# Moving the split weights 16 bytes against the activations in a two-layer decoder trunk

## The chip, the cores and the metric

The kernel runs on one core of one Trainium2 chip. The metric is the device time of one execution in microseconds (us). The median of three runs of the kernel before is 1382.09 us (1382.05 to 1382.2).

## What is computed

Two residual layers on x of 256 tokens by 1024 channels, batch 1, all in float32:

```
h = rms_norm(x)
layer 0: p = h @ w_in_ab; gMLP gating on some columns, dilated attention on the others
         x = x + concat(...) @ w_out_ab
         x = x + (silu(h' @ wg) * (h' @ wu)) @ wd             # width 2816
layer 1: p = h @ w_in_cd; block attention (12 heads) and a short convolution
         x = x + concat(...) @ w_out_cd
         out = sum over 8 experts of gate[:, e] * swiglu(h', wg[e], wu[e], wd[e])   # width 3584
         x = x + out                                          # each token has 2 of 8 gates
```

The last stage is the largest: eight experts, three matrices each of 1024 x 3584 floats.

## The kernel before, in words

**Three products for one.** A matmul of plain float32 operands is replaced by three with operands of the type float32r. Each weight tile and each activation is split in a high part (a copy rounded to float32r) and a low part (the rest). `three` (L724 to L728) issues high x high (L726), high x low (L727) and low x high (L728) into the same PSUM bank. Its first operand is the stationary one (128 columns, loaded by LDWEIGHTS), the second the moving one. In the profile's rows the moving operand is named first: `psum<-w_hi,xg_hi` has weights moving, activations stationary.

**The weights' way.** SP loads tiles of 4096 floats a partition (2 MB) into `raw_ring`, which has 7 slots, in a fixed order (L547 to L581). A tile is worked on in four units of 1024 floats. For each unit ACT writes the high part into `w_hi` (L388; L409 in the expert stage), DVE subtracts it and writes the low part into `w_lo` (L396, L414), and PE multiplies. `w_hi` and `w_lo` have 4 buffers each; ACT waits until PE has used the unit four before (`unit_used`), and SP reloads a slot when DVE has split its last unit (`lo_ready`).

**Who multiplies what.** In the projections (`project`, L788; `first_tile`, L762), the output projections (`ab_unit`, `out_units`, `out_last`) and the down product of the feed-forward (`down`, L1185) 512 (at times 256) columns of weights move past 128 stationary columns of `act` or `ffn_h`. The feed-forward reads its input from `ffn_in_hi/lo`: at its opening (L1199 to L1210) it is stationary and 512 columns of weights move; from then on (L1213 to L1227) 128 columns of weights are stationary and 256 columns of `ffn_in` move. The convolution (`conv_half`, L1005) is of that second form, with `act` moving. In the expert stage (`job`, L1320; eight jobs, one for each expert, of 7 gate, 7 up and 7 down tiles) 512 columns of weights move, and `xg` (128 gathered tokens) or `moe_hT` is stationary. There `transpose_h` (L1307) turns the hidden rows with transposes whose moving operand is the identity, in `const`; `gather` (L1290) does so with `xg_rows`.

**Where things lie.** All addresses in SBUF are laid out by hand. `keep` (L190) places buffers one behind the other and rounds each up to 32 bytes; `at` gives an address outright:

```
        raw = keep("raw_ring", [RING, TILE])
        wh = keep("w_hi", [SPLITS, UNIT], F32R)
        wl = keep("w_lo", [SPLITS, UNIT], F32R)
        xres = keep("x_residual", [TT, D])
        cst = keep("const", [C_COLS])
...
        R0 = place[0] + PHASE + 256
        act_hi = at("act_hi", [KD, SEQ], F32R, R0)
        ffn_hi = at("ffn_in_hi", [KD, SEQ], F32R, R0 + FFN_PHASE)
```

`xg` and `moe_h` start at R0 plus multiples of 4096, and `ffn_h`, `moe_hT`, `xg_rows`, `probs` at R0 plus 16384 plus multiples of 256. Each step of a loop over k, c or a buffer number moves an operand by a multiple of 256 bytes, so two operands keep their distance modulo 256 bytes through a whole stage.

From the start of `raw_ring` to R0 there are 169,952 bytes of buffers, plus PHASE = 32, plus 256: 170,240, which is 665 x 256. `w_hi` starts 114,688 = 448 x 256 bytes behind that start. So activations and weights lie at the same place modulo 256, and `ffn_in` (FFN_PHASE = -192) 64 bytes past them.

Of the kernel before, what the change touches and what calls it, by code (L numbers as in the profile page):

```python
# [24 lines left out]
F32R = mybir.dt.float32r  # L25
# [26 lines left out]
UNIT = 1024  # L52
SPLITS = 4
# [1 line left out]
SLAB = 512  # L55


PHASE, FFN_PHASE = 32, -192
SLABS = FE // SLAB
JOB_TILES = 3 * SLABS  # L60
JOB_UNITS = JOB_TILES * TILE // UNIT
# [109 lines left out]
def decoder_trunk(nc, x, norm_mix, norm_ffn, w_in_ab, gmlp_v_gain, gmlp_ws, gmlp_bs, dil_q_gain, dil_k_gain,  # L171
# [10 lines left out]
    with ExitStack() as ctx:  # L182
# [4 lines left out]
        def at(name, shape, dt, offset):  # L187
            return nc.alloc_sbuf_tensor_at(name, [P, *shape], dt, offset=offset)

        def keep(name, shape, dt=F32):  # L190
            size = int(np.prod(shape)) * (2 if dt == BF16 else 4)
            t = at(name, shape, dt, place[0])
            place[0] += (size + 31) // 32 * 32
            return t

        raw = keep("raw_ring", [RING, TILE])
        wh = keep("w_hi", [SPLITS, UNIT], F32R)
        wl = keep("w_lo", [SPLITS, UNIT], F32R)
        xres = keep("x_residual", [TT, D])
        cst = keep("const", [C_COLS])  # L200
        colpar = keep("col_params", [48])
# [2399 lines left out]
```

## Time and profile before

| | |
|---|---|
| median of three runs | 1382.09 us |
| profiled execution, its own time | 1382.9 us |
| its span, first to last instruction | 1381.1 us |
| PE busy | 1366.9 us (99%) |
| DVE busy | 1194.4 us (86%) |
| ACT busy | 1026.2 us (74%) |
| read from HBM | 425.09 MB, 313 GB/s over the span |

The profile gives each engine's busy time. The matmuls are pipelined, and each one's duration holds its way through the array, so they overlap: 512 columns show 389 to 394 ns while the next one starts 227 ns later. For the pace of TensorE the starts of neighbours in the timeline are to be read, not the durations. PEld is the load of stationary operands, beside PE.

### The profile page before, as it was taken

How to read it: one execution, taken by the hardware profiler on the slowest of the kernel's cores; microseconds unless marked ns; L12 is line 12 of the kernel's file. 1: busy time of each engine (PE TensorE's matmuls, PEld its weight loads, DVE VectorE, ACT ScalarE, POOL GpSimd, SP SyncE). 2: the span in 40 equal slices, each digit the busy share in tenths (PEclk: the TensorE clock that was granted, in tenths of full speed). 3: DMA queues.
4: the chain of work that ended last, by engine and by line, in shares of the span. 5: the costliest groups of instructions: out<-in, count | busy, mean ns of one | idle time of the engine just before them, and what ended most of it. 6: DMA issues, size and time to landing. Idle time of an engine off the chain costs nothing.

```text
span 1381.1 us, 20276 instructions
## 1 busy us (share of the span) xinstructions
PE 1366.9 (99%) x6985; PEld 1150.9 (83%) x6985; DVE 1194.4 (86%) x1517; ACT 1026.2 (74%) x1262; POOL 86.2 (6%) x67
## 2 busy tenths in 40 slices
PE   9999999999999999999999999999999999999998
PEld 7778999988988788888888888888888888888886
DVE  5876555568959999999999999999999999999998
ACT  5666444456758788888887887888888888888877
POOL 1020000000320000000100100010010001001000
PEclk9999999999999999999999999999999999999999
DMA  9944543643658999999999999999999999999980
GB/s 347 356 151 154 183 153 122 231 136 122 245 183 331 362 375 348 391 392 377 357 394 380 342 396 393 377 355 393 382 352 394 389 376 354 393 376 351 394 328 30
DMA packets 183760, 430.28 MB, mean 312 GB/s; under 512 B 5449, under 2 KB 13301, under 8 KB 183712
## 3 DMA queue, kind: packets, MB, share of 16 engines
q1 hardware_dynamic: 181408, 423.86, 82.7%
q0 software_dynamic: 2304, 5.78, 2.1%
q8 instruction: 30, 0.49, 0.1%
q14 instruction: 18, 0.15, 0.0%
HBM read 425.09 MB, written 7.34 MB: 313 GB/s over the span
## 4 chain that ended last, share of the span: by engine, by line
PE 93%; DVE 5%; ACT 1%; issue 1%; DVEq 0%; ACTq 0%
PE psum L726 29%; PE psum L728 29%; PE psum L727 29%; PE psum L1313 2%; DVE w_lo L414 1%; DVE w_lo L396 1%; PE psum L1294 0%; PE psum L758 0%; PE psum L1157 0%; PE psum L859 0%; DVE probs L2078 0%; PE psum L1000 0%; PE psum L891 0%; PE psum L877 0%; PE psum L968 0%
## 5 line engine op out<-in xcount | busy, mean ns | idle before, releaser
L414 DVE TENSOR_TENSOR w_lo<-raw_ring,w_hi 128x1024 fp32r<-128x1024 f32 x674 | 812.3, 1223 | 48.3 <-ACT w_hi L409 4.0
L409 ACT ACTIVATE w_hi<-raw_ring 128x1024 fp32r<-128x1024 f32 x675 | 715.3, 1063 | 169.0 <-PE psum L728 168.4
L726 PE MATMUL psum<-w_hi,xg_hi 128*128 128x512 f32 x896 | 353.4, 394 | 1.1 <-DVE w_lo L414 1.0
L728 PE MATMUL psum<-w_hi,xg_lo 128*128 128x512 f32 x896 | 349.3, 390 | 0.0
L727 PE MATMUL psum<-w_lo,xg_hi 128*128 128x512 f32 x896 | 348.9, 389 | 0.0
L396 DVE TENSOR_TENSOR w_lo<-raw_ring,w_hi 128x1024 fp32r<-128x1024 f32 x124 | 151.7, 1230 | 78.7 <-ACT w_hi L388 77.7
L388 ACT ACTIVATE w_hi<-raw_ring 128x1024 fp32r<-128x1024 f32 x124 | 129.9, 1057 | 95.1 <-PE psum L728 94.9
L728 PEld LDWEIGHTS psum<-w_hi,xg_lo 128*128 128x128 f32 x896 | 168.2, 188 | 35.7
L726 PEld LDWEIGHTS psum<-w_hi,xg_hi 128*128 128x128 f32 x896 | 168.3, 188 | 34.9 <-issue 1.4
L727 PEld LDWEIGHTS psum<-w_lo,xg_hi 128*128 128x128 f32 x896 | 168.4, 188 | 33.6
L726 PE MATMUL psum<-w_hi,moe_hT_hi 128*128 128x512 f32 x448 | 176.1, 393 | 0.1
L728 PE MATMUL psum<-w_hi,moe_hT_lo 128*128 128x512 f32 x448 | 174.6, 390 | 0.0
L727 PE MATMUL psum<-w_lo,moe_hT_hi 128*128 128x512 f32 x448 | 174.3, 389 | 0.0
L728 PEld LDWEIGHTS psum<-w_hi,moe_hT_lo 128*128 128x128 f32 x448 | 84.1, 188 | 17.9
L726 PEld LDWEIGHTS psum<-w_hi,moe_hT_hi 128*128 128x128 f32 x448 | 84.1, 188 | 17.4 <-issue 0.5
L727 PEld LDWEIGHTS psum<-w_lo,moe_hT_hi 128*128 128x128 f32 x448 | 84.2, 188 | 17.1
L726 PE MATMUL psum<-w_hi,act_hi 128*128 128x512 f32 (+1 forms) x224 | 86.0, 384 | 2.9 <-DVE w_lo L396 2.1
L728 PE MATMUL psum<-w_hi,act_lo 128*128 128x512 f32 (+1 forms) x224 | 84.0, 375 | 0.0
L727 PE MATMUL psum<-w_lo,act_hi 128*128 128x512 f32 (+1 forms) x224 | 83.9, 374 | 0.0
L726 PE MATMUL psum<-ffn_in_hi,w_hi 128*128 128x256 f32 x288 | 80.9, 281 | 0.0
L727 PE MATMUL psum<-ffn_in_lo,w_hi 128*128 128x256 f32 x288 | 80.4, 279 | 0.0
L728 PE MATMUL psum<-ffn_in_hi,w_lo 128*128 128x256 f32 x288 | 80.4, 279 | 0.0
(286 smaller groups left out, 1355.9 us busy)
## 6 DMA issues: line engine op xcount, KB each, us to landing
raw_ring<-in_moe_w_gate SPq DMA_DIRECT2D x56, 2048.0 KB, 10.3
raw_ring<-in_moe_w_up SPq DMA_DIRECT2D x56, 2048.0 KB, 10.8
raw_ring<-in_moe_w_down SPq DMA_DIRECT2D x56, 2048.0 KB, 10.7
raw_ring<-in_ffn_w_gate SPq DMA_DIRECT2D x5, 2048.0 KB, 7.9
raw_ring<-in_ffn_w_up SPq DMA_DIRECT2D x5, 2048.0 KB, 9.3
raw_ring<-in_ffn_w_down SPq DMA_DIRECT2D x5, 2048.0 KB, 10.1
raw_ring<-in_w_in_ab SPq DMA_DIRECT2D x4, 2048.0 KB, 16.2
raw_ring<-in_w_in_cd SPq DMA_DIRECT2D x4, 2048.0 KB, 8.0
```

The source lines that it names most:

```text
L388: act.activation(part(wh, u, w), raw_unit(u), ACT.Copy).then_inc(hi_ready, 1)
L396: dve.tensor_tensor(part(wl, u, w), raw_unit(u), part(wh, u, w).bitcast(F32), ALU.subtract).then_inc(lo_ready, 1)
L409: act.activation(wh[:, v % SPLITS, :], moe_raw(i, q), ACT.Copy).then_inc(hi_ready, 1)
L414: dve.tensor_tensor(wl[:, v % SPLITS, :], moe_raw(i, q), wh[:, v % SPLITS, :].bitcast(F32), ALU.subtract).then_inc(lo_ready, 1)
L726: pe.matmul(out_, sh, mh_, start=start, stop=False)
L727: pe.matmul(out_, sh, ml_, start=False, stop=False)
L728: return pe.matmul(out_, sl, mh_, start=False, stop=stop)
L1313: mm = pe.transpose(ps[:, 4, c * P:(c + 1) * P], mh[:, i % 2, c * P:(c + 1) * P], ident)
```

## The change

`w_hi` and `w_lo` become slices of one allocation, `w_split`, that begin LINE = 4 floats (16 bytes) into it. With 4 floats of padding at either end it is 32 bytes longer than the two were, so all that `keep` places behind it (`x_residual`, `const`, the parameters, the masks) lies 32 bytes further on. PHASE goes from 32 to 0, which makes up for it: R0 stays where it was. FFN_PHASE goes from -192 to -128: `ffn_in` moves up by 64 bytes. No instruction is added, removed or reordered.

```
-PHASE, FFN_PHASE = 32, -192
+PHASE, FFN_PHASE, LINE = 0, -128, 4
...
-        wh = keep("w_hi", [SPLITS, UNIT], F32R)
-        wl = keep("w_lo", [SPLITS, UNIT], F32R)
+        split = keep("w_split", [2 * SPLITS * UNIT + 2 * LINE], F32R)
+        wh = split[:, LINE:LINE + SPLITS * UNIT].rearrange("p (s f) -> p s f", s=SPLITS)
+        wl = split[:, LINE + SPLITS * UNIT:LINE + 2 * SPLITS * UNIT].rearrange("p (s f) -> p s f", s=SPLITS)
```

Starts modulo 256 bytes, counted from the start of `raw_ring`:

| | before | after |
|---|---|---|
| `raw_ring` | 0 | 0 |
| `w_hi`, `w_lo` | 0 | 16 |
| `x_residual`, `const` | 0 | 32 |
| `act`, `xg`, `moe_h`, `moe_hT`, `ffn_h` | 0 | 0 |
| `ffn_in` | 64 | 128 |
| `act`, `xg`, `moe_hT`, `ffn_h` less weights | 0 | -16 |
| `ffn_in` less weights | +64 | +112 |

## Rows read from the trace of the kernel before

**Rows 1.** The page: span, busy time, share and instructions of each engine

```profile
span 1381.1 us, 20276 instructions
PE 1366.9 (99%) x6985; PEld 1150.9 (83%) x6985; DVE 1194.4 (86%) x1517; ACT 1026.2 (74%) x1262; POOL 86.2 (6%) x67
```

**Rows 2.** The page: the chain that ended last, by engine

```profile
PE 93%; DVE 5%; ACT 1%; issue 1%; DVEq 0%; ACTq 0%
```

**Rows 3.** Groups by line, shapes apart, weights moving: busy us, mean ns | idle before

```profile
L726 PE MATMUL psum<-w_hi,xg_hi 128*128 128x512 f32 x896 | 353.4, 394 | 1.1 <-DVE w_lo L414 1.0
L726 PE MATMUL psum<-w_hi,moe_hT_hi 128*128 128x512 f32 x448 | 176.1, 393 | 0.1
L726 PE MATMUL psum<-w_hi,act_hi 128*128 128x512 f32 x192 | 76.7, 399 | 2.9 <-DVE w_lo L396 2.1 <-issue 0.8
L726 PE MATMUL psum<-w_hi,ffn_h_hi 128*128 128x512 f32 x88 | 34.5, 392 | 0.0
L726 PE MATMUL psum<-w_hi,ffn_in_hi 128*128 128x512 f32 x32 | 12.8, 399 | 0.2 <-DVE ffn_in_lo L1880 0.2
```

**Rows 4.** The same view, weights stationary or 256 columns, and the transposes

```profile
L726 PE MATMUL psum<-ffn_in_hi,w_hi 128*128 128x256 f32 x288 | 80.9, 281 | 0.0
...
L726 PE MATMUL psum<-act_hi,w_hi 128*128 128x256 f32 x48 | 14.5, 303 | 0.2 <-ACT p_v L1673 0.2
...
L726 PE MATMUL psum<-w_hi,act_hi 128*128 128x256 f32 x32 | 9.3, 290 | 0.0
...
L1313 PE MATMUL psum<-const,moe_h 128*128 128x128 f32 x224 | 33.5, 271 | 0.0
```

**Rows 5.** PE timeline, expert stage: start us, us; 14 evenly spaced matmuls between

```profile
902.75 0.39 PE L726 MATMUL psum<-w_hi,xg_hi 128*128 128x512 f32 x1
...
906.15 0.39 PE L726 MATMUL psum<-w_hi,xg_hi 128*128 128x512 f32 x1
```

**Rows 6.** PE timeline, the feed-forward's opening; 16 matmuls between

```profile
119.82 0.39 PE L727 MATMUL psum<-w_lo,ffn_in_hi 128*128 128x512 f32 x1
...
123.79 0.39 PE L726 MATMUL psum<-w_hi,ffn_in_hi 128*128 128x512 f32 x1
```

**Rows 7.** PE timeline, feed-forward with stationary weights; 26 matmuls between

```profile
137.78 0.28 PE L728 MATMUL psum<-ffn_in_hi,w_lo 128*128 128x256 f32 x1
...
140.96 0.28 PE L728 MATMUL psum<-ffn_in_hi,w_lo 128*128 128x256 f32 x1
```

**Rows 8.** PE timeline, convolution; 9 matmuls between

```profile
379.14 0.28 PE L727 MATMUL psum<-act_lo,w_hi 128*128 128x256 f32 x1
...
380.34 0.28 PE L728 MATMUL psum<-act_hi,w_lo 128*128 128x256 f32 x1
```

**Rows 9.** Timeline, all engines: a matmul and the next load of a stationary operand

```profile
902.98 0.39 PE L727 MATMUL psum<-w_lo,xg_hi 128*128 128x512 f32 x1
902.98 0.19 PEld L728 LDWEIGHTS psum<-w_hi,xg_lo 128*128 128x128 f32 x1
```

**Rows 10.** PE timeline: four transposes in the expert stage and what follows

```profile
914.32 0.60 PE L1313 MATMUL psum<-const,moe_h 128*128 128x128 f32 x4
914.67 0.48 PE L726 MATMUL psum<-w_hi,xg_hi 128*128 128x512 f32 x1
```

**Rows 11.** Three stretches of the expert stage: length, then busy us by engine

```profile
600.00:800.00 200.00, 200.00 (x918) 165.79 (x918) 189.63 (x195) 164.75 (x184) 15.79 (x6) 1.00 1.02 373
800.00:1000.00 200.00, 200.00 (x915) 165.77 (x914) 188.98 (x192) 162.95 (x176) 9.57 (x4) 1.00 1.03 382
1000.00:1200.00 200.00, 200.00 (x915) 165.71 (x913) 190.14 (x199) 164.95 (x186) 14.16 (x5) 1.00 1.02 376
```

**Rows 12.** Groups by line from 600 to 1200 us: the two splits

```profile
L414 DVE TENSOR_TENSOR w_lo<-raw_ring,w_hi 128x1024 fp32r<-128x1024 f32 x425 | 513.0, 1224 | 31.3 <-ACT w_hi L409 1.8
L409 ACT ACTIVATE w_hi<-raw_ring 128x1024 fp32r<-128x1024 f32 x424 | 449.5, 1063 | 105.7 <-PE psum L728 105.4
```

**Rows 13.** The page: DMA issues, KB each, us to landing

```profile
raw_ring<-in_moe_w_gate SPq DMA_DIRECT2D x56, 2048.0 KB, 10.3
```

**Rows 14.** POOL groups: a write that starts 4 bytes off, and one that doesn't

```profile
L665 POOL TENSOR_TENSOR conv_y<-conv_y,row_params 128x255 f32<-128x255 f32 x2 | 1.5, 772 | 0.2
...
L637 POOL TENSOR_TENSOR p_uv<-p_uv,small 128x256 f32<-128x256 f32 x2 | 1.2, 615 | 47.6 <-DVE small L2019 47.5
```

## The prediction, made before the changed kernel was run

> **What bounds the kernel now.** I read the busy shares first, then the chain, the groups, and at last the timeline. TensorE is busy for 1366.9 of 1381.1 us [rows 1], and 93% of the chain that ended last is PE [rows 2]. Its groups hardly wait: the largest, 896 matmuls, idled 1.1 us in all [rows 3]. In three stretches of 200 us of the expert stage PE has no gap, at granted clock 1.00, that is 2.4 GHz [rows 11]. So the time is the number of matmuls times the distance from one start to the next, and only that distance can be moved by a change that adds and removes no instruction.
>
> The durations don't show it, the starts do. Between the two matmuls of [rows 5] lie 15 distances in 3.40 us: 226.7 ns for 512 columns. With 256 columns and the same placement it is 1.20 us for 10, 120.0 ns [rows 8]. The difference, 106.7 ns for 256 columns, is the pure cost of a column (0.417 ns, one cycle at 2.4 GHz); both forms carry 13.3 ns on top. The kernel before happens to hold other placements too. At the opening of the feed-forward the same form of matmul reads a stationary operand 64 bytes past the weights, and takes 3.97 us for 17 distances, 233.5 ns [rows 6]: 6.8 ns more, 20.2 on top. Later the weights are stationary and the input moves, so that the stationary one lies 64 bytes short: 3.18 us for 27, 117.8 ns [rows 7], 2.2 ns less than [rows 8], 11.1 on top. The load of the next stationary operand starts in the same hundredth of a microsecond as the matmul that it runs beside [rows 9], so both read SBUF together. Below, "distance" of an address is that of the stationary operand less that of the moving one, modulo 256.
>
> **The change, part by part.**
>
> (a) Weights moving, 512 columns, distance from 0 to -16 bytes. [Rows 3] has 896 + 448 + 192 + 88 triples whose stationary operand moves by this: 1624 x 3 = 4872 matmuls. At 226.7 ns they are 1104 us, 80% of the span, all of it on the path. No row has -16. The price comes from the neighbours: from 0 to +64 it rises by 6.8 ns, 0.106 ns a byte; carried on to the other side, 16 bytes give -1.7 ns. From 0 to -64 (256 columns) it falls by only 2.2 ns, so the line must flatten somewhere; evenly spread, 16 bytes would give -0.55 ns, and -2.2 at once if it is a step. I take -1.7, from the rows of the same form: -8.3 us. Ends: -2.2 ns, -10.7 us, and, since nothing excludes that 0 is the best place, the +6.8 ns of the worst row, +33.1 us.
>
> The Trainium skill (TensorE: Matmul & The Clock Gate, Step-by-step: what each phase is for) says that the moving and the stationary operand have a read port each and that the load takes no bandwidth from the running matmul. By that rule the change is worth nothing; this trace speaks against it, since 226.7 and 233.5 ns stand for one form of matmul at two placements.
>
> (b) The feed-forward's opening, distance from +64 to +112: 32 x 3 = 96 matmuls [rows 3]. The same line gives +5.1 ns, +0.5 us. Ends: -0.7 us (back to the 226.7 of [rows 5]) and +1 us (twice the line).
>
> (c) The rest of the feed-forward, weights stationary, distance from -64 to -112: 288 x 3 = 864 matmuls of 256 columns [rows 4]. The nearest row is their own, 117.8 ns; I take no change. Ends: another 48 bytes at 2.2 / 64 ns each, -1.4 us; or the 20.2 ns on top of [rows 6] instead of 11.1, +9.1 ns, +7.9 us.
>
> (d) Convolution, 48 x 3 with the distance from 0 to +16, and 32 x 3 projection matmuls of 256 columns with -16 [rows 4]: 144 x 1.7 = +0.2 us and 96 x 1.7 = -0.2 us, together nothing; no more than 1.3 us either way at 6.8 and 2.2 ns.
>
> (e) Transposes move the identity, in `const`, which goes 32 bytes up, while most of their stationary operands stay: four of them lie in 0.35 us to the next matmul [rows 10]. There are 224 of this line [rows 4], and I count about 420 in all. Zero, since nothing in the trace prices their placement; 6.8 ns each would be +2.9 us, 2.2 ns each -0.9 us.
>
> (f) ACT's and DVE's splits read `raw_ring` at 0 and write 16 bytes past a multiple of 32. They lie beside PE. From 600 to 1200 us DVE is busy for 189.63 + 188.98 + 190.14 = 568.8 of 600 us [rows 11], 425 splits in it [rows 12]: 1338 ns a unit against PE's 1412. So 74 ns more on each split of 1224 cost nothing, and PE 5.2% faster would still be fed. Below that cover each further ns costs one on some 670 units. The only rows with a start off 32 bytes are POOL's, 772 ns for 255 elements against 615 for 256 in another operation [rows 14], on an engine whose times are rough. A quarter more on DVE's split would add 306 - 74 = 232 ns a unit, +155 us; I take zero, as POOL's two rows are different operations.
>
> (g) DMA: SP's loads don't move. A tile takes 10.3 us to land [rows 13] and is asked for up to seven tiles ahead, and a tile is 4 x 1.41 = 5.6 us of PE; a pace 0.7% faster asks for 380 GB/s where the stretches show 373 to 382 [rows 11]. Cover stays.
>
> Sum: -8.3 + 0.5 + 0 + 0 = -7.8 us. Against the profiled execution's own 1382.9 us that is 1375.1; the median of the runs is 0.8 lower, so I forecast 1374.3 us. Own range 1371 to 1379.
>
> **The rivals.**
>
> *Zero is the best place* (slower). What costs the 13.3 ns may be smallest where both reads start in step, and rise to both sides. For it: +64 is dearer. Against it: -64 isn't, though with half the columns. It decides as soon as a start-to-start distance in the expert stage is above 227.3 ns (0.2% of the run spread over 4872). Price: 1.7 ns the other way is +8.3 us, 1390 us, and up to 1415 at the 233.5 ns of [rows 6].
>
> *A larger step down.* The 13.3 ns on top may be a meeting of the two reads at the same place, which a shift of 16 bytes avoids in large part. Half of it gone would be -6.7 ns, -32.6 us, 1350 us. For it: with 11.1, 13.3 and 20.2 the amount does depend on placement. Against it: 64 bytes short saved only 2.2. DVE's 5.2% of cover would just hold (6.7 of 226.7 is 3.0%).
>
> By the Trainium skill (TensorE: Matmul & The Clock Gate, Back-to-back issue gap) a matmul of 512 columns costs 512 / 2.4 + 2.5 = 215.8 ns; 10.9 ns less on 4872 would be -53 us, some 1329 us, an estimate from that page alone. The rows here show nothing below 11.1 ns on top.
>
> *It does nothing.* The cost might go by coarser steps than 16 bytes, so that -16 reads like 0: 1382 us. For it: the trace shows only distances in steps of 64. Against it: +64 and -64 differ from 0 in both directions, so there is a slope somewhere. The rule of the Trainium skill cited under (a) (TensorE: Matmul & The Clock Gate, Step-by-step: what each phase is for) gives this same time.
>
> *DVE becomes the bound* by the placement in (f): over 1400 us. Nothing but POOL's rows speaks for it.
>
> **How the numbers follow.** Forecast 0.40; larger step down 0.15; nothing, or within 0.2% (2.8 us, about what a measurement of this kernel tells from no change), 0.17; zero is best 0.25; DVE 0.03. Faster by over 0.2% is 0.40 + 0.15 = 0.55, the same 0.17, slower 0.28. The 8-in-10 range reaches down into the larger step, to 1354, and up through +8.3 us to about +3 ns a matmul, 1397; some 0.07 lies below and 0.12 above.
>
> **What would show it.** Right: starts in the expert stage 225.0 ns apart where they were 226.7, the opening of the feed-forward at about 238, its later part still near 118, splits still 1224 and 1063 ns, PE without gaps. Wrong: 228 ns or more in the expert stage (zero was best), 222 or less (a larger step), a PE that waits for `w_lo` with splits over 1300 ns (f), or gains in the expert stage given back in the feed-forward (c).

## The result, and the profile after

The changed kernel takes 1404.1 us (1404.01 to 1404.47, 5 runs) against 1382.2 us for the kernel before in the same session: a ratio of 1.0158, 95% interval 1.0147 to 1.0168. It is 22 us slower; the prediction said 8 us faster, range 1354 to 1397.

The page of the changed kernel; the lines of the source stand one lower than before, and both split buffers now carry the name `w_split`:

```profile
span 1402.7 us, 20276 instructions
PE 1389.1 (99%) x6985; PEld 1154.6 (82%) x6985; DVE 1195.6 (85%) x1517; ACT 1026.9 (73%) x1262; POOL 59.0 (4%) x67
...
PE 94%; DVE 4%; ACT 1%; issue 1%; DVEq 0%; ACTq 0%
...
L727 PE MATMUL psum<-w_split,xg_hi 128*128 128x512 f32 x896 | 357.2, 399 | 0.9 <-DVE w_split L415 0.8
...
raw_ring<-in_moe_w_gate SPq DMA_DIRECT2D x56, 2048.0 KB, 10.2
```

The same count of instructions, PE on 94% of the chain where it was 93%, and no wait of PE that was not there in [rows 1 to 3]. The splits, by line over the stretch from 600 to 1200 us:

```profile
L415 DVE TENSOR_TENSOR w_split<-raw_ring,w_split 128x1024 fp32r<-128x1024 f32 x417 | 504.1, 1223 | 40.3 <-ACT w_split L410 33.5
L410 ACT ACTIVATE w_split<-raw_ring 128x1024 fp32r<-128x1024 f32 x416 | 441.3, 1064 | 113.8 <-PE psum L729 113.0
```

1223 and 1064 ns against 1224 and 1063 [rows 12]: ACT and DVE don't notice the 16 bytes. They wait more, ACT on PE and DVE on ACT. The same three stretches as in [rows 11], with busy us and number of instructions of each engine:

```profile
600.00:800.00 200.00, 200.00 (x900) 163.17 (x899) 186.66 (x192) 161.74 (x181) 6.72 (x6) 1.00 1.01 367
800.00:1000.00 200.00, 200.00 (x898) 163.05 (x897) 186.01 (x191) 160.42 (x175) 5.08 (x4) 1.00 1.01 375
1000.00:1200.00 200.00, 200.00 (x899) 163.03 (x898) 187.25 (x196) 161.84 (x181) 5.09 (x5) 1.00 1.01 369
```

The granted clock is 1.00 (2.4 GHz) as before and PE has no gap, but it starts 900, 898 and 899 matmuls where it started 918, 915 and 915. So each is further from the next. In the PE timeline (start us, us) of the expert stage, with 15 evenly spaced matmuls between:

```profile
910.79 0.40 PE L727 MATMUL psum<-w_split,xg_hi 128*128 128x512 f32 x1
...
914.50 0.40 PE L728 MATMUL psum<-w_split,xg_hi 128*128 128x512 f32 x1
```

3.71 us for 16 distances, 231.9 ns, against 226.7 [rows 5]. The feed-forward's opening (19 matmuls between) and its later part (29 between):

```profile
119.19 0.39 PE L729 MATMUL psum<-w_split,ffn_in_lo 128*128 128x512 f32 x1
...
123.86 0.39 PE L728 MATMUL psum<-w_split,ffn_in_hi 128*128 128x512 f32 x1
...
149.82 0.28 PE L728 MATMUL psum<-ffn_in_lo,w_split 128*128 128x256 f32 x1
...
153.42 0.28 PE L728 MATMUL psum<-ffn_in_lo,w_split 128*128 128x256 f32 x1
```

4.67 us for 20 is 233.5 ns, exactly [rows 6]; 3.60 us for 30 is 120.0 ns, 2.2 more than [rows 7].

Read to the nanosecond, the starts show more. All 6985 matmuls come in the same order in both kernels, so their start times can be subtracted one by one: the changed kernel is 0.6 us late at the end of layer 0's mixer, 0.5 after the opening of the feed-forward, 3.4 at its end, 4.4 at the start of the expert stage, and 21.6 at its end. In that stage the distances are not random. Once a few matmuls have passed behind a break, before the change they go 227, 226, 227 without end, and after it 235, 235, 230, 227, 235, 235, 230, 227: a cycle of four matmuls, mean 231.7. The few matmuls of run-in cost the kernel before some 36 ns in each of 57 stretches, and the changed kernel 2 ns.

### The profile page after: what moved, and what is told of

Read it like the earlier page. It is cut to its first block, busy times and chain, and to the rows that moved or that the text cites. A ratio compares the mean times of both kernels' runs of the same rounds, so it can differ in the third digit from the quotient of the medians.

```text
span 1402.7 us, 20276 instructions
## 1 busy us (share of the span) xinstructions
PE 1389.1 (99%) x6985; PEld 1154.6 (82%) x6985; DVE 1195.6 (85%) x1517; ACT 1026.9 (73%) x1262; POOL 59.0 (4%) x67
## 4 chain that ended last, share of the span: by engine, by line
PE 94%; DVE 4%; ACT 1%; issue 1%; DVEq 0%; ACTq 0%
PE psum L727 30%; PE psum L729 29%; PE psum L728 29%; PE psum L1314 2%; DVE w_split L397 1%; PE psum L1295 0%; PE psum L759 0%; PE psum L1158 0%; PE psum L860 0%; DVE probs L2079 0%; PE psum L1001 0%; PE psum L892 0%; DVE rope_tmp L466 0%; DVE p_qk L468 0%; DVE rope_tmp L460 0%
## 5 line engine op out<-in xcount | busy, mean ns | idle before, releaser
L415 DVE TENSOR_TENSOR w_split<-raw_ring,w_split 128x1024 fp32r<-128x1024 f32 x674 | 813.7, 1223 | 63.6 <-ACT w_split L410 52.6
L410 ACT ACTIVATE w_split<-raw_ring 128x1024 fp32r<-128x1024 f32 x675 | 715.8, 1064 | 185.5 <-PE psum L729 184.4
L727 PE MATMUL psum<-w_split,xg_hi 128*128 128x512 f32 x896 | 357.2, 399 | 0.9 <-DVE w_split L415 0.8
L729 PE MATMUL psum<-w_split,xg_lo 128*128 128x512 f32 x896 | 353.3, 394 | 0.0
L728 PE MATMUL psum<-w_split,xg_hi 128*128 128x512 f32 x896 | 353.1, 394 | 0.0
L397 DVE TENSOR_TENSOR w_split<-raw_ring,w_split 128x1024 fp32r<-128x1024 f32 x124 | 151.4, 1227 | 82.6 <-ACT w_split L389 81.7
L389 ACT ACTIVATE w_split<-raw_ring 128x1024 fp32r<-128x1024 f32 x124 | 130.3, 1058 | 99.2 <-PE psum L729 98.8
L729 PEld LDWEIGHTS psum<-w_split,xg_lo 128*128 128x128 f32 x896 | 168.5, 188 | 39.0
L727 PEld LDWEIGHTS psum<-w_split,xg_hi 128*128 128x128 f32 x896 | 168.6, 188 | 38.2 <-issue 1.3
L728 PEld LDWEIGHTS psum<-w_split,xg_hi 128*128 128x128 f32 x896 | 168.7, 188 | 37.1
L727 PE MATMUL psum<-w_split,moe_hT_hi 128*128 128x512 f32 x448 | 178.0, 397 | 0.1
L729 PE MATMUL psum<-w_split,moe_hT_lo 128*128 128x512 f32 x448 | 176.6, 394 | 0.0
L728 PE MATMUL psum<-w_split,moe_hT_hi 128*128 128x512 f32 x448 | 176.6, 394 | 0.0
L727 PEld LDWEIGHTS psum<-w_split,moe_hT_hi 128*128 128x128 f32 x448 | 84.3, 188 | 19.2 <-issue 0.5
L728 PEld LDWEIGHTS psum<-w_split,moe_hT_hi 128*128 128x128 f32 x448 | 84.3, 188 | 18.8
L727 PE MATMUL psum<-w_split,act_hi 128*128 128x512 f32 (+1 forms) x224 | 86.5, 386 | 2.5 <-DVE w_split L397 1.6
L728 PE MATMUL psum<-w_split,act_hi 128*128 128x512 f32 (+1 forms) x224 | 84.6, 378 | 0.0
```

What stands on the lines that cost most here:

```text
L389: act.activation(part(wh, u, w), raw_unit(u), ACT.Copy).then_inc(hi_ready, 1)
L397: dve.tensor_tensor(part(wl, u, w), raw_unit(u), part(wh, u, w).bitcast(F32), ALU.subtract).then_inc(lo_ready, 1)
L410: act.activation(wh[:, v % SPLITS, :], moe_raw(i, q), ACT.Copy).then_inc(hi_ready, 1)
L415: dve.tensor_tensor(wl[:, v % SPLITS, :], moe_raw(i, q), wh[:, v % SPLITS, :].bitcast(F32), ALU.subtract).then_inc(lo_ready, 1)
L727: pe.matmul(out_, sh, mh_, start=start, stop=False)
L728: pe.matmul(out_, sh, ml_, start=False, stop=False)
```

## The experiments

In the kernels among them the activations or the weights are moved by constants only; instructions and their order stay. The four runs of TensorE alone (`map512`, `map256`, `breaks`, `breaks256`) leave the whole computation out. Where an activation had to lie off 32 bytes, it became a slice of a buffer that begins lower, as the change does it for the weights. Below, a placement is written (moving, stationary), both starts in bytes modulo 256 counted from `raw_ring`. Where 512 columns of weights move past `act`, `xg`, `moe_hT` or `ffn_h`, the kernel before is (0, 0) and the changed one (16, 0). "Stretch" is a run of matmuls of one form between two transposes or other breaks.

**Weights or distance?**

```
act_back16  -PHASE, FFN_PHASE = 32, -192          +PHASE, FFN_PHASE = 16, -176
both_up16   -PHASE, FFN_PHASE, LINE = 0, -128, 4  +PHASE, FFN_PHASE, LINE = 16, -192, 4
act_up16    -PHASE, FFN_PHASE = 32, -192          +PHASE, FFN_PHASE = 48, -192
act_back64  -PHASE, FFN_PHASE = 32, -192          +PHASE, FFN_PHASE = -32, -128
```

> The kernel before with the activations moved instead of the weights: weights at 0 modulo 256, all operands of the activations 16 bytes lower (distance -16 as after the change), ffn_in kept 64 bytes past the weights as before. Distance theory (only stationary less moving counts): 231.7 ns from start to start in the expert stage as after the change, feed-forward opening 233.5 and its later part 117.8 as before; about 1382 + 20 = 1402 us. Line-start theory (weights that begin off a multiple of 32 bytes are dear to stream): 226.7 ns and 1382 us, as the weights are back on 0. If any operand off 32 bytes costs: also near 1402, so the next run has to tell.

Measured: 1383.13 us, ratio to before 1.0002 (0.9993 to 1.0012). The very distance of the change, with the weights at 0, costs next to nothing: by the start times 0.7 us in the expert stage, where 37 of 57 stretches run at 226.7 ns and 20 at 228.3. That fells the distance theory.

> The kernel after with the activations moved up by 16 bytes too and ffn_in put at +64 less the weights: everything 16 bytes past 0, distance 0. Distance theory: 226.7 ns in the expert stage, 117.8 in the feed-forward, 1382 us. Line-start theory, for weights or for any operand: 231 ns or more, 1400 us or more.

Measured: 1398.02 us, ratio 1.011 (1.0093 to 1.0127). Distance 0, but everything 16 bytes up, and the expert stage goes at 231.8 ns in the mean. Yet the later part of the feed-forward, at (80, 16), ran at 113.3 ns, 4.5 less than in the kernel before, on stationary weights that begin at 16. So weights off 32 bytes are not dear where they stay; for weights that move, the line-start theory still stands here, and w16_act160 below decides on it.

> The kernel before with activations 16 bytes higher (distance +16; ffn_in at +80). Distance theory with 0 as the best place: between 226.7 and 231.7 if the cost rises evenly to +64 (about 228.4 by the line of 0.106 ns a byte), or 231.7 if both sides are alike; 1390 to 1404 us.

Measured: 1405.35 us (one run). At (0, 16) the expert stage holds both 226.7 and 233.3 ns. In its PE timeline, 50 matmuls at even pace stand between the first two rows, 33 between the last two:

```profile
914.73 0.39 PE L736 MATMUL psum<-w_lo,xg_hi 128*128 128x512 f32 x1
...
926.63 0.39 PE L736 MATMUL psum<-w_lo,xg_hi 128*128 128x512 f32 x1
926.86 0.39 PE L737 MATMUL psum<-w_hi,xg_lo 128*128 128x512 f32 x1
927.09 0.60 PE L1322 MATMUL psum<-const,moe_h 128*128 128x128 f32 x4
927.45 0.47 PE L735 MATMUL psum<-w_hi,xg_hi 128*128 128x512 f32 x1
...
928.21 0.39 PE L735 MATMUL psum<-w_hi,xg_hi 128*128 128x512 f32 x1
...
935.92 0.39 PE L736 MATMUL psum<-w_lo,moe_hT_hi 128*128 128x512 f32 x1
```

11.90 us for 51 distances is 233.3 ns; then come four transposes; then 7.71 us for 34, 226.8 ns. The placement is the same on both sides (the last row is already a down product, with `moe_hT` at 16 like `xg`). The pace changed across the transposes. Inside a stretch, behind its first few matmuls, it changes in none of the 57 of this run. This is the key of the study: a placement can have two paces, and a break can lead from one to the other.

> The kernel before with activations 64 bytes lower (distance -64; ffn_in kept at +64). If the expert stage follows the 256-column rows (2.2 ns less at -64 than at 0), 224.5 ns and about 1371 us. If 0 is the best place and -16 cost 5.0 ns, more than 231.7 ns at -64, 1404 us or more. If the cost depends on multiples of 64 only for the placement of lines, 226.7 ns and 1382 us.

Measured: 1390.64 us (one run), 228.8 to 228.9 ns in all 57 stretches of the expert stage. None of the three numbers.

**TensorE alone.** Next the disputed cost was measured by itself.

> A kernel of its own that leaves the whole computation out: TensorE alone multiplies triples as in the expert stage (512 columns move, 128 are stationary, low parts 16384 and 4096 bytes behind the high ones), 27 matmuls for each of 16 x 16 placements of the moving and the stationary operand in steps of 16 bytes modulo 256, with ACT, DVE and the loads silent. If the cost is made by TensorE's own two reads and hangs on both starts, the map shows the kernels' own paces: 226.7 ns for (moving 0, stationary 0), 231 to 232 for (16, 0) and (16, 16), 232.5 for (0, 16), 228 for (0, 240), 229 for (0, 192), 233.3 for (0, 64), and there are placements below 226. If it is made by ACT's and DVE's accesses beside it, all 256 places give one number, 226.7 or less. If only the distance counts, rows of equal distance agree.

> The same for the form of the feed-forward and the convolution: 128 columns of weights stationary, 256 of the activations moving. If TensorE's own two reads make the cost: 119.7 ns for (moving 0, stationary 0), 117.8 for (64, 0), 119.5 to 119.9 for (128, 16) and (80, 0), 113.4 for (80, 16). If ACT and DVE make it: one number throughout.

Measured: ACT and DVE are silent, DVE is busy for 7.3 us in all, and the paces are there all the same:

```profile
span 1664.4 us, 14478 instructions
...
PE 1642.4 (99%) x7216; PEld 1337.8 (80%) x7216; DVE 7.3 (0%) x1; ACT 13.1 (1%) x15; POOL 0.2 (0%) x4
```

(16, 0) shows 234, 235, 230, 228, the changed kernel's own cycle. (16, 16) shows 228, 232, mean 230.0, which is the pace of 10 of the 57 stretches of both_up16; the others have paces that the next run shows. Some rows of the maps, ns from start to start, mean of 24 distances behind one break:

```
512 columns move    stationary at
moving at     0    16    48    64    80   112   128   160   192   240
    0     227.7 226.7 233.2 233.3 232.0 233.3 233.3 233.3 229.5 228.0
   16     231.5 230.0 227.3 234.7 226.8 227.1 233.2 226.7 231.2 232.2
   64     229.5 231.8 227.7 228.3 233.5 233.2 233.3 233.9 232.2 230.2
  192     233.3 232.3 233.4 232.1 233.3 229.8 228.9 233.4 226.7 233.2

256 columns move
    0     119.9 118.3 122.7 114.0 118.8 120.3 118.8 120.0 117.8 119.9
   16     113.6 117.9 119.8 118.8 113.9 116.6 116.7 114.9 118.1 118.2
   64     117.8 116.7 117.2 119.5 118.3 117.8 114.0 118.8 118.5 118.1
  192     114.0 118.8 119.6 118.6 119.8 118.1 117.8 116.8 119.4 118.3
```

Along a row of the map only the address of the load of the stationary operand differs, down a column only that of the moving one, and the pace changes with either, so both reads have a part in it. A cell is one draw, but the next run confirms this on many: (0, 0), (0, 64) and (16, 0) keep apart in all their stretches. The loads themselves take 187 to 190 ns at every placement of the first form. Two cells missed their forecast clearly: (0, 16) gave 226.7 where 232.5 was expected, and (80, 16) of the second form 118.3 where 113.4 was. The places below 226 ns that were expected are not there either.

Of 256 placements of the first form 12 are under 227.0 and 117 over 233; none is under 226.7. The first form's best is 226.7 / 512, the second's 113.3 / 256: 0.443 ns a column in both, 17/16 of the cycle of 0.417 ns.

**Does a break choose?**

> TensorE alone again, the computation left out: ten placements (moving, stationary), each with 28 stretches of 21 matmuls, and before each stretch a break (one matmul of 64 to 172 columns, every other time behind four transposes). If the start-to-start distance is fixed by the placement, all 28 stretches of a placement settle at one pace. If a break can throw the two reads into another standing pattern, some placements show two or more paces: (0, 16) 226.7 and 233, (0, 240) 226.7 and 228.5, while (0, 0) always comes back to 226.7 and (16, 0) never does (231.7).

Measured, mean of the last 12 distances of each of 28 stretches:

```
placement    paces (stretches)                the kernels' expert stage, stretches of 20 and more
(0, 0)       226.7 to 227.6 (28)              before: 226.7 (57)
(16, 0)      231.6 to 231.7 (28)              after: 231.7 (57)
(0, 240)     228.3 (20), 226.7 (8)            act_back16: 226.7 (37), 228.3 (20)
(0, 16)      233.2, 233.3 (22), 226.7 (6)     act_up16: 233.3 (49), 226.7 (8)
(16, 16)     230.0 (12), 233.3 (12), 231 (4)  both_up16: 231.1 (25), 233.3 (22), 230.0 (10)
(0, 192)     228.8, 228.9 (27), 233.3 (1)     act_back64: 228.9 (57)
(16, 160)    231 (18), 226.7 (10)             w16_act160: 231.1 (34), 226.7 (23)
(0, 64)      233.3 (28)
(80, 96)     236.7 (21), 233.3 (5), 226.7 (2)
(192, 192)   227.5 to 227.7 (15), 226.7 (13)
```

Each kernel runs at the paces that its placement has when TensorE is alone, and at no others; how often it has each differs. (0, 0) always returns to its fast pace (the values up to 227.6 still hold some of the run-in of a stretch of 21), (16, 0) never finds one.

**Three checks inside the kernel.**

```
w16_act160   +PHASE, FFN_PHASE, LINE = 160, -208, 4
after_ffn80  +PHASE, FFN_PHASE, LINE = 0, -176, 4
ffn_up16     +PHASE, FFN_PHASE = 32, -240
```

> The kernel after, weights still at 16, with the activations at 160 and ffn_in at 208. By the maps (moving 16, stationary 160) is 226.7 ns, so the expert stage is as fast as before although the weights begin off 32 bytes; later part of the feed-forward (moving 208, stationary 16) 115.0: 1380 us. If weights at 16 are dear in themselves: 230 ns or more, 1398 us or more.

Measured: 1388.97 us, ratio 1.0046 (1.0031 to 1.0061). Weights at 16 as in the changed kernel, and 16 us of its 22 are gone, by the start times 7.7 before the expert stage and 8.4 in it, where 23 of 57 stretches run at 226.7 and the rest at 231.1. So weights that move from 16 can be streamed at the best pace, and the line-start theory falls too. The opening of the feed-forward, at (16, 208), runs at 226.7 where both kernels had 233.3, and its later part at 113.6. The forecast of 1380 us was missed by 9. The map alone promised too much, since each of its cells is one draw.

> The kernel after with one part undone: ffn_in back to 64 bytes past the weights (that is, at 80), all else as after the change. Expert stage unchanged at 231.7 ns; later part of the feed-forward at 113.4 (as when both lay 16 up) instead of 119.8, 864 matmuls, -5.5 us: 1398.6 us. If (80, 16) falls into its other pattern, 118.4: 1403 us. My first theory (distance alone) gives 117.8, 1402.4 us.

Measured: 1401.61 us, ratio 1.014 (1.0123 to 1.0157), between the two forecasts, and by the start times 3.0 us less than the changed kernel. The expert stage stays at 231.7, so the feed-forward's input is a small part of the loss. The later part ran at 113.3 ns until the first down products came between; the 256-column stretches after them ran at 118.3. In the timeline, 29 matmuls between these two rows of the fast part:

```profile
152.02 0.28 PE L736 MATMUL psum<-ffn_in_hi,w_split 128*128 128x256 f32 x1
...
155.42 0.28 PE L736 MATMUL psum<-ffn_in_hi,w_split 128*128 128x256 f32 x1
```

3.40 us for 30 distances, 113.3 ns. So a change of form can be a break too.

> The kernel before with ffn_in alone moved, from 64 to 16 bytes past the weights; everything else as before. By the maps: later part of the feed-forward at 113.6 ns (moving 16, stationary 0) instead of 117.8, 864 matmuls, -3.6 us; its opening at 226.7 (moving 0, stationary 16) instead of 233.3, 96 matmuls, -0.6 us: 1378 us. If the pace also hangs on the break before, the later part could stay at 118 to 120: 1382 to 1384 us. By my first theory (a line through +64 at 0.106 ns a byte, later part the dearer the nearer to 0) the later part goes to 119.4: 1383 us.

Measured: 1383.18 us, ratio 1.0002 (0.9993 to 1.0011). A miss: 116.7 at first, 118.7 from the first down products on, the opening 233.3. One draw of a map is no forecast.

**Stretches of the second form, and two last placements.**

> TensorE alone, the form of the feed-forward (weights stationary, 256 columns move), 16 stretches of 21 matmuls behind breaks for each of 20 placements: the moving operand at 0, 16, ... 240 with weights at 0, then (80, 16), (128, 16), (208, 16), (144, 16). If standing patterns chosen by the break are the rule here too: (64, 0) 117.8 in nearly all stretches, (16, 0) both 113.4 and 116.7, (80, 16) both 113.4 and 118.4, (128, 16) 119.5 to 119.9; a placement with weights at 0 whose stretches all come out near 114 would save about 3 us in the kernel. If one number belongs to each placement, (16, 0) shows 113.6 alone and the 116.7 of the last kernel stays unexplained.

Measured, 16 stretches each, weights at 0: (64, 0) 117.8 (15), 113.3 (1); (16, 0) 116.7 (6), 118.4 to 118.8 (10); (192, 0) 113.3 (12), 117.8 (4); (112, 0) 113.3 to 115.0 (16). With weights at 16: (80, 16) 118.3 (9), 113.3 (7); (128, 16) 120.0 (11), 118.3 (5); (208, 16) 113.3 (15), 114.2 (1). The 116.7 and 118.7 of ffn_up16 are there, as are both paces of after_ffn80.

```
ffn_up192   -PHASE, FFN_PHASE = 32, -192   +PHASE, FFN_PHASE = 32, -64
ffn_up112   -PHASE, FFN_PHASE = 32, -192   +PHASE, FFN_PHASE = 32, -144
```

> The kernel before with ffn_in alone moved, to 192 past the weights. From the stretches behind breaks (moving 192, stationary 0: 113.3 ns in 12 of 16, 117.8 in 4): later part of the feed-forward 113.3 to 114.4 ns where it was 117.8, 864 matmuls, -2.9 to -3.9 us; opening (moving 0, stationary 192) 229 instead of 233.3, 96 matmuls, -0.4 us; 1378.4 to 1379.4 us, faster than both kernels. If the break in front of it picks the other pattern: 117.8, 1382.3 us. By the distance line of the prediction (192 less than 256 is 64 short for the opening, 64 past for the later part): later part dearer, 1386 us.

Measured: 1381.32 us, ratio 0.9992 (0.9983 to 1.0001). 113.4 ns before the first down products, 117.8 in everything behind them: both paces of (192, 0), the slow one for longer. The forecast of 1378.4 to 1379.4 was missed, and the interval doesn't tell the time from the kernel before; by the start times it gains 1.3 us.

> ffn_in alone moved, to 112 past the weights, the distance that the change gives it, but with the weights left at 0. From the stretches: later part (moving 112, stationary 0) 113.3 to 115.0 in all 16, -2.4 to -3.9 us; opening (moving 0, stationary 112) 233.3 as before; 1378.5 to 1380 us. After the change the same distance with weights at 16 took 119.9 ns: if only the distance counted, this one would take 119.9 too and 1384.6 us.

Measured: 1379.14 us, ratio 0.9975 (0.9966 to 0.9985): faster than both kernels. 113.7 ns in the mean of the whole later part, 3.8 us gained there by the start times, the opening still 233.3. The distance is the changed kernel's own +112; only the weights' 16 bytes are missing, and 120.0 ns have become 113.7.

## Why the prediction was wrong

**What bounds the kernel** was right: PE's start-to-start distance and nothing else. Splits, loads and clock did not move, as (f) and (g) had it.

**(a), the step that failed.** It took the extra over a column's bare cost as a function of one number, stationary less moving, and laid a line of 0.106 ns a byte through two placements 64 bytes apart. It forecast -1.7 ns, -8.3 us, on 4872 matmuls; inside a stretch they measured +5.0 (226.7 to 231.7). With the run-in behind each break the mean of the 3900 unbroken distances of the expert stage went from 227.30 to 231.71 ns, +4.4: 17.2 us, and the start times show the same. All 4872 together lost 20.0 us, 4.1 ns each. Two things are wrong in the step. The two starts count each for itself: distance -16 is 231.7 ns at (16, 0) and 226.7 or 228.3 at (0, 240), and distance 0 is 226.7 at (0, 0) and 230.0 to 233.3 at (16, 16). And there is no slope: in the map, neighbours 16 bytes apart differ by up to 10 ns, with no order that a line could follow. The stage's even 226.7 in [rows 5], against 233.5 in [rows 6], was two points of a scatter.

The step had a warning that I saw and talked away: the row at -64 contradicted the line by a factor of three. It also had an end of +33 us and a reason for it; a likeliest value should not have been taken from a line that its own third row refuted. That 226.7 and 120.0 ns "both carry 13.3 on top" was chance as well: the best stretches cost 17/16 cycle a column in either form, 13.3 ns on 512 and 6.7 on 256, so (0, 0) was at the lowest pace measured in the first form and far from it in the second. At none of the placements tried had the expert stage anything to win.

**(b)** forecast +0.5 us; the opening stayed at 233.5 ns, 0 us. **(c)** forecast no change; 117.9 became 120.0 ns, 864 matmuls, 1.8 us, and the start times put 2.9 us on the feed-forward behind its opening, down products included, which pay like the expert stage. **(d)** nothing, right in size: the convolution went from 119.4 to 118.2 ns in the mean, 0.2 us. **(e)** right in size: the transposes of the expert stage start 108.7 ns apart where it was 108.3. Of transposes that move the identity there are some 490, not 420; with a price of nothing that changes no sum.

**The rivals.** "Zero is the best place" had the sign and its trigger of 227.3 ns, and its span from 1390 to 1415 holds the time. Its reason was not the right one: with the weights on 0 the same distance costs next to nothing (act_back16), and with both at the same 16 (both_up16) distance 0 is dear. "DVE becomes the bound" and "it does nothing" are out. "A larger step down" found nothing: no placement of 256 is below 226.7.

The two-port rule of the Trainium skill (TensorE: Matmul & The Clock Gate, Step-by-step: what each phase is for) is contradicted by the maps, in which TensorE works alone and the pace goes from 226.7 to 236.7 ns with the two addresses. The gap of 215.8 ns by the Trainium skill (TensorE: Matmul & The Clock Gate, Back-to-back issue gap), which that section gives for an isolated matmul, was reached by none of the placements of float32r operands.

What in the memory makes the standing patterns is not shown here: the runs show that TensorE's own work suffices and that both starts count, not where or why the two reads meet, nor why a break leads to one pace and not to another.

## What to carry to other kernels

Where TensorE is the bound with back-to-back matmuls, read the start-to-start distance of each form against its best (here 17/16 cycle a column): a constant surplus of some per cent can be the placement of the two operands. Don't extrapolate it from neighbours. Measure many short stretches behind breaks for each placement, on TensorE alone. Prefer a placement whose every stretch is fast to one that is fast only at times. And a buffer that is moved for one stage moves in all of them: the 16 bytes were paid on 4872 matmuls, 20 us.

## What the runs showed of the hardware that was not expected

- A matmul of 128 x 128 by 512 float32r columns, with a new stationary operand each time, starts 226.7 to 236.7 ns after the last at granted clock 1.00, by where the two operands begin, tried in steps of 16 bytes over 256; with 256 columns it is 113.3 to 122.7 ns.
- The pace is a standing cycle of two to four or more matmuls (235, 235, 230, 227; 228, 232), and some placements have two or three. It holds over 50 matmuls and more, until transposes or another form break it, and may then be another: 233.3 and 226.8 ns on either side of four transposes.
- ACT's and DVE's splits have no part in it: TensorE alone shows the same paces. Nor do they feel their own placement: 1064 and 1223 ns whether their output begins on 32 bytes or 16 past.
